# Layer 1's branch gates as 512-column products with the low blocks beside the high ones

## The reference, cut to what matters

```python
proj = h @ w_in[l]
...
def merge_branches(gate_in, y_att, y_conv, y_sc, w_o):
    g_att, g_conv, g_sc = jnp.split(jax.nn.sigmoid(gate_in), N_BRANCH, axis=-1)
    return (g_att * y_att + g_conv * y_conv + g_sc * y_sc) @ w_o
...
x = x + g1 * merge_branches(proj[..., SC_END:GATE_END], att, y_conv, y_sc, w_o[l])
```

## Time and profile before

| | us |
|---|---|
| median of three runs | 1224.73 |
| profiled execution | 1224.44 |
| its span | 1222.7 |
| TensorE busy | 1202.3 (98%) |
| VectorE busy | 864.9 (71%) |
| ScalarE busy | 530.0 (43%) |
| GpSimd busy | 190.4 (16%) |

### The profile page before, as it was taken

How to read it: one execution, slowest core, us unless ns; L and a number is a source line. 1 busy time by engine, 2 the same in 40 slices (tenths; PEclk the granted TensorE clock), 3 DMA queues, 4 the chain that set the end, 5 groups by cost and what they waited for, 6 DMA issues and landing times.

```text
span 1222.7 us, 17823 instructions
## 1 busy us (share of the span) xinstructions
PE 1202.3 (98%) x6842; PEld 1000.4 (82%) x6842; DVE 864.9 (71%) x1286; ACT 530.0 (43%) x891; POOL 190.4 (16%) x158
## 2 busy tenths in 40 slices
PE   7999999999999999999999999999999999999997
PEld 5677777788888898888888888889879998888886
DVE  4665866586877487678755665789887877766666
ACT  4342555522433352312232222465664555655554
POOL 0005994000001200000000000302980002000000
PEclk9999999999999999999999999999999999999999
DMA  9947322134464536557664665335434674676662
GB/s 297 314 142 216 84 54 69 35 87 121 120 172 124 169 92 198 159 156 215 185 201 144 211 195 161 93 98 147 124 111 115 168 209 141 195 200 189 181 198 88
DMA packets 265252, 188.88 MB, mean 154 GB/s; under 512 B 16035, under 2 KB 250833, under 8 KB 265169
## 3 DMA queue, kind: packets, MB, share of 16 engines
q1 hardware_dynamic: 264832, 187.60, 52.6%
q10 hardware_dynamic: 337, 0.15, 0.0%
HBM read 186.67 MB, written 1.05 MB: 154 GB/s over the span
## 4 chain that ended last, share of the span: by engine, by line
PE 87%; DVE 4%; ACT 3%; DMA 2%; issue 1%; DVEq 0%; ACTq 0%; SPq 0%
PE bank L2075 17%; PE bank L2077 17%; PE bank L2076 17%; PE bank L2116 5%; PE bank L2114 3%; PE scores L2563 3%; PE bank L2543 2%; PE bank L2545 2%; PE bank L2544 2%; PE probsT L2572 2%; PE attended L2586 1%; ACT Whi L401 1%; DMA Wraw<-in_w_in 1%; DVE Wlo L412 1%; PE bank L2642 1%
## 5 line engine op out<-in xcount | busy, mean ns | idle before, releaser
L412 DVE TENSOR_TENSOR Wlo<-Wraw,Whi 128x1024 fp32r<-128x1024 f32 (+3 forms) x294 | 321.7, 1103 | 105.4 <-ACT Whi L401 104.3
L401 ACT ACTIVATE Whi<-Wraw 128x1024 fp32r<-128x1024 f32 (+1 forms) x296 | 270.3, 928 | 127.0 <-PE bank L2077 71.6
L2075 PE MATMUL bank<-Hhi,Whi 128*128 128x512 f32 (+1 forms) x786 | 285.9, 364 | 0.4
L2076 PE MATMUL bank<-Hlo,Whi 128*128 128x512 f32 (+1 forms) x786 | 282.1, 359 | 0.0
L2077 PE MATMUL bank<-Hhi,Wlo 128*128 128x512 f32 (+1 forms) x786 | 282.0, 359 | 0.0
L2075 PEld LDWEIGHTS bank<-Hhi,Whi 128*128 128x128 f32 x786 | 148.6, 189 | 29.1 <-issue 6.4
L2076 PEld LDWEIGHTS bank<-Hlo,Whi 128*128 128x128 f32 x786 | 148.6, 189 | 22.3 <-issue 1.0
L2077 PEld LDWEIGHTS bank<-Hhi,Wlo 128*128 128x128 f32 x786 | 148.6, 189 | 21.9
L2075 PE MATMUL bank<-Uhi,Whi 128*128 128x512 f32 (+1 forms) x350 | 128.5, 367 | 0.2 <-issue 0.2
L2077 PE MATMUL bank<-Uhi,Wlo 128*128 128x512 f32 (+1 forms) x350 | 126.8, 362 | 0.0
L2076 PE MATMUL bank<-Ulo,Whi 128*128 128x512 f32 (+1 forms) x350 | 126.7, 362 | 0.0
(11 more groups left out here) (305 smaller groups left out, 1979.4 us busy)
## 6 DMA issues: line engine op xcount, KB each, us to landing
Wraw<-in_w_ff SPq DMA_DIRECT2D x126, 512.0 KB, 3.9
Wraw<-in_w_in SPq DMA_DIRECT2D x78, 512.0 KB, 4.0
ATT<-in_w_mod SPq DMA_DIRECT2D x58, 512.0 KB, 4.5
Wraw<-in_w_o SPq DMA_DIRECT2D x16, 512.0 KB, 4.0
ACC<-in_w_mod SPq DMA_DIRECT2D x14, 512.0 KB, 4.6
Wraw<-in_w_mla_o SPq DMA_DIRECT2D x8, 512.0 KB, 4.1
ATT<-in_w_mod SPq DMA_DIRECT2D x12, 256.0 KB, 7.6
Wraw<-in_w_kv_b SPq DMA_DIRECT2D x12, 256.0 KB, 3.7
```

The costliest lines, as they stand in the source:

```text
L401: last = act.activation(hi, raw, ACT.Copy)
L412: last = eng.tensor_tensor(lo, raw, hi.bitcast(F32), ALU.subtract)
L2075: pe.matmul(dst, sh, mh, start=j == 0, stop=False)
L2076: pe.matmul(dst, sh, ml, start=False, stop=False)
```

## The change

In layer 1 only: ScalarE copies the eight low blocks of `h` into the second half of `Hhi`, two blocks an instruction, one instruction at each of the four steps of the attention's output product. TensorE's gate tiles become `tile_beside` tiles, 8 matmuls of 512 columns and 8 of 256 in place of 24 of 256. ScalarE copies the second half of the bank to `TG`'s second half, VectorE adds the bank's first half, and ScalarE takes the tanh of that sum into `TG`'s first half. The tanh of g0 stands behind ScalarE's `look` for g1, the tanh of g1 behind the copy of g1.

```diff
@@ ScalarE
                 for m in range(4):
+                    if l:
+                        act.activation(Hhi[:, 2 * m:2 * m + 2, half[1]], Hlo[:, 2 * m:2 * m + 2, half[0]].bitcast(F32),
+                                       ACT.Copy).then_inc(beside, 1)
...
+                def gate_side(j):
+
+                    t = at.tile()
+                    act.wait_ge(tile_done, t.done)
+                    act.activation(TG[:, j, half[1]], banks[t.bank][:, half[1]], ACT.Copy).then_inc(side_done, 1)
+                    return t
+
+                def gate_tanh_out(t, j):
+
+                    act.wait_ge(drained[t.bank], t.drained)
+                    act.activation(TG[:, j, half[0]], TG[:, j, half[1]], ACT.Tanh, scale=0.5).then_inc(branch_tanh, 1)
...
-                    before = outs[-2:]
+                    before, gates = outs[-2:], []
                     for j in range(2):
                         look(next(nxt))
+                        if j and l:
+                            gate_tanh_out(gates[0], 0)
                         if before:
                             act.wait_ge(drained[before[j].bank], before[j].drained)
-                        copy_out(TG[:, j, 0:TQ], TQ, ACT.Tanh, 0.5)
+                        if l:
+                            gates.append(gate_side(j))
+                        else:
+                            copy_out(TG[:, j, 0:TQ], TQ, ACT.Tanh, 0.5)
                         if j == MEAN_AFTER[l] and mean:
                             mean()
                         if j == 0 and squares:
                             squares()
+                    if l:
+                        gate_tanh_out(gates[1], 1)
@@ VectorE
                     for j in range(2):
                         look_and_fold(next(nxt))
                         gates.append(at.tile())
+                        if l:
+                            dve.wait_ge(side_done, sides.next())
+                            dve.tensor_tensor(TG[:, j, half[1]], banks[gates[j].bank][:, half[0]], TG[:, j, half[1]],
+                                              add).then_inc(drained[gates[j].bank], 1)
...
-                        dve.wait_ge(drained[gates[j].bank], gates[j].drained)
+                        if l:
+                            dve.wait_ge(branch_tanh, tanhs.next())
+                        else:
+                            dve.wait_ge(drained[gates[j].bank], gates[j].drained)
@@ TensorE
                     for j in range(2):
-                        tile_of(P, DT, H, 0, TQ)
+                        if l:
+                            pe.wait_ge(beside, 4)
+                            tile_beside()
+                        else:
+                            tile_of(P, DT, H, 0, TQ)
```

More of the change, by code:

```diff
@@ L330, in build @@
         side_done = sem("side_done")
+        beside = sem("beside")
+        branch_tanh = sem("branch_tanh")
         value_gated = sem("value_gated")
@@ L1745, in _ @@
                 outs = []
+                sides, tanhs = Tally(), Tally()
                 looked = 0
@@ L1893, in hidden_block @@
                     low(Ulo[:, u, 0:TQ], PR[:, j, 0:TQ], Uhi[:, u, 0:TQ])
-                sides = Tally()
                 def gate_sum(j, free):
```

## The result

The changed kernel takes 1230.18 us (median of five runs, 1229.62 to 1231.65) against 1224.73 of the kernel before (1224.48 to 1225.72): 5.45 us more, ratio 1.0044 with a 95% interval of 1.0033 to 1.0055. The forecast was 1230.6, slower. The profiled execution took 1229.62 us, the shortest of the five; its span is 1227.8 us, 5.1 more than before.

What follows compares the result with a forecast made beforehand. TensorE, busy 98%, bounds the kernel; its 1.3 us saving would vanish inside waits for VectorE and ScalarE, whose shifts reach 6.2 us at the second output block. So 1224.44 + 6.2 = 1230.6 us, range 1228 to 1232.7.

Steps and rivals of the forecast that it cites:

- copies beside: Four ScalarE copies in the attention's output product, inside its waits for TensorE: cost 0; bare, 2.5 us.
- scaling of ACC: VectorE's last instruction before the mean over channels, groups 0 and 1: from 958.11 to about 959.4, shift 1.3 us.
- low weights of group 4, shift of its tile: VectorE's low weights for g0 of group 4 move from 970.86 to 973.7; TensorE's tile starts 2.8 us later.
- one loop, groups 5 to 7: VectorE and ScalarE's loop per group: 6.7 us, 0.5 more if a load is late, then 7.4 and 7.4.
- low part of the second output block: VectorE's instruction that TensorE's second output block waits for: from 1001.60 to 1007.8, total shift 6.2 us.
- term of 0.5 us for a late load: In the first of three loops of groups 5 to 7: 0.5 us more where a load lands late.
- term of 0.08 us a tile: TensorE's gate tiles fall from 2.88 to 2.80 us: 0.08 a tile, 1.3 us for the stage's 16.
- after it nothing is changed: After the branches' output product, which waits for VectorE and ScalarE in the same order, nothing changes.
- (A): Rival: TensorE keeps the bound, adds and tanhs lie in VectorE's and ScalarE's idle time; 1223.1 us, chance 0.10.
- (B): Rival: late mean, cheaper chain through g1's tanh, only VectorE's own order counts; 1226.0 to 1227.2 us, chance 0.17.
- the detour: g1's next weight copy queues behind ScalarE's tanh, which waits for VectorE's sum: 1.2 us each time.
- (C): Rival: loads come to bound, groups 4 to 7 each wait 0.5 to 1 more; 1232.6 to 1234.6 us, chance 0.13.

Runs made afterwards that it cites:

- no_low_sum: The changed kernel with ScalarE's tanh straight from the bank's first half and no VectorE sums, low operand's part left out: 1224.01 us against 1225.25 before.
- fitted_product: As fitted, but VectorE takes the convolution's product ahead of group 3's second output; operand copies stay: 1224.21 us against 1224.63 before.
- tanh_late: The changed kernel with ScalarE's tanh of g1 moved behind the next group's g1 weight copy: 1225.88 us against 1225.25 before.
- before_fitted: The kernel before with only the respread taps and split normalisation on VectorE, none of the change: 1225.62 us against 1224.97 before.
- fitted: The change with g1's tanh behind the weight copy, two taps ahead of the sum, taps respread, normalisation split: 1225.23 us against 1224.97 before.
- fitted_conv: As fitted, with VectorE's convolution product ahead of group 3's second output and ScalarE's operand copy behind group 4's weight copies: 1225.21 us against 1224.76.

## Why the prediction was right

The forecast held by its own steps, which can be read against the trace after, since the stretch starts within 0.06 us of where it did.

| step of the prediction | forecast | measured |
|---|---|---|
| gate tile | 2.80 | g0 2.81, g1 2.78 (940.40, 943.21, 945.99) |
| copies beside | in ScalarE's waits, last ends 938.9 | ends 938.71 |
| first taps | after 943.9 | 944.17 |
| scaling of ACC | 959.4 | 959.19 |
| low part of g1's weights, group 3 | 966.7 | 966.51 |
| reciprocal | 970.45 | 970.23 |
| low weights of group 4, shift of its tile | 973.7, 2.8 | 973.46, 2.65 |
| ScalarE idle ahead of g1's tanh | up to 2.7 | 2.75 |
| branch operand's tile | 981.8 | 981.55 |
| low weights of group 5, shift | 982.8, 4.4 | 982.56, 4.20 |
| low part of g1's weights, group 5 | 985.8 | 985.56 |
| one loop, groups 5 to 7 | 6.7 or 7.2, 7.4, 7.4 | 6.72, 7.38, 7.37 |
| low part of the second output block | 1007.8, shift 6.2 | 1007.03, shift 5.43 |

*The copies cost nothing.* They took 0.61 to 0.63 us each, 2.5 in all, and ScalarE's wait for TensorE in that place fell from 7.0 to 4.9 us; the last is done at 938.71, 1.7 us before the first gate tile. The first and the last of the four in ScalarE's timeline:

```profile
931.01 0.63 ACT L1036 ACTIVATE Hhi<-Hlo 128x512 fp32r<-128x512 f32 x1
...
938.10 0.61 ACT L1036 ACTIVATE Hhi<-Hlo 128x512 fp32r<-128x512 f32 x1
```

*What was mis-sized.* The term of 0.5 us for a late load in the first of the three loops didn't come: no wait of ScalarE for a load is left between 972 and 1008, where the kernel before had four from 972 to 1003; the chunks are copied later than before, and find their loads landed. The three loops took 21.47 us, not 22.0. With the 0.2 us by which each earlier step was early this makes the 0.8 of 6.2 that is missing.

*What the tiles save.* The term of 0.08 us a tile held. In TensorE's timeline the first group's two gate tiles take 5.59 us (940.40 to 945.99), where they took 5.76 (940.46 to 946.22): 0.085 a tile. First the end of before, then the changed kernel:

```profile
946.22 0.28 PE L2075 MATMUL bank<-Uhi,Whi 128*128 128x256 f32 x1
```

```profile
940.40 0.40 PE L2142 MATMUL bank<-Hhi,Whi 128*128 128x512 f32 x1
...
943.21 0.40 PE L2142 MATMUL bank<-Hhi,Whi 128*128 128x512 f32 x1
...
945.99 0.28 PE L2104 MATMUL bank<-Uhi,Whi 128*128 128x256 f32 x1
```

A whole group falls from 7.20 us to 7.01 (940.40 to 947.41), so eight groups would give 1.5 us if nothing were waited for; no_low_sum gets 1.05 of it. (*The Trainium skill (TensorE: Matmul & The Clock Gate, "Back-to-back issue gap") would give 0.02 a tile by its isolated gap, an estimate; the tile distances here give some four times as much.*) In the changed kernel all of it is lost in waits.

*What was not forecast.* Ahead of the mean, the gate row's second half waited 0.24 us for a bank that VectorE's late `G += Z` frees. The mean itself moved by 1.07 (958.78 to 959.85), not by 1.3, because the scaling of ACC that it waits for moved by 1.08 (958.11 to 959.19). And "after it nothing is changed" left out the 0.35 us that come back at a tile of the FFN.

*The rivals.* (A) would hold if TensorE kept the bound; fitted_product comes nearest to that, and gives 0.4 in the medians and 0.8 in the stage where (A) had 1.3. (B) put only VectorE's own order on the path, 1.6 to 2.8 us over the kernel before: tanh_late takes the detour out and lands at +0.63 in both counts, under that range. Counted without the form's 1.05, which is in it, VectorE's own order costs some 1.7 us there, and the detour 4.9 more. (C) is excluded by the missing load waits.

*Where luck has a part.* By the steps the forecast was too high: by 0.8 at the second output block, and by 1.0 for the profiled execution, from which it was summed (1230.6 against 1229.62). That it meets the median within 0.5 us is owed in part to the changed kernel's profiled execution being the shortest of five, 0.56 under their median.

*The waits as a sum.* Taken from the distances of matmul starts, TensorE is held 1.78, 0.92, 0.81 and 1.45 us at the last four waits, each 0.15 to 0.16 more than the idle time that the rows give: idle time counts from the modelled end of the matmul before, 0.28 after its start, where the next could have started after 0.12. That is 4.96, of which 0.27 stood before too; around the gate row and the mean 1.45 is added, which makes 6.1. Less 1.5, what the tiles save where nothing waits, 4.6 of the 5.49 are told. The rest is in tiles that start late or follow a late start. Where TensorE had waited for low weights the first gate tile takes 2.99 and 3.00 us, not 2.81 (974.78 to 977.77, 983.89 to 986.89), 0.37 in all, and smaller steps of up to 0.1 at other tiles of the stage make up the other 0.5. The rows name no wait for any of this, and its cause is not shown.

What stays open: by how much a version of fitted_product with more rounds beats the kernel before; the stage says 0.77, the medians 0.42 with an interval of some 1.1 to either side. And why the whole profiled span of before_fitted is 3.1 us longer than before's, when its stage is 1.0 longer: 2.5 of it lie ahead of the stage, which starts at 931.37 there and at 928.85 before. Its profiled execution is its longest, and its median is 0.65 above.

## What to carry to other kernels

When a result is handed from ScalarE to VectorE and back, look at what stands behind the waiting instruction on each queue before counting instructions: here 32 small instructions more cost 0.3 to 0.6 us of the stage in the better orders (77.16 against 76.88 without them, in an order of its own; 78.25 against 77.64 in the same order), and the place of one tanh ahead of a weight copy cost 4.9 us. Put the waiting instruction behind the work that others need sooner, and read the other engine's idle time in front of that work (here 1.43 us each round) as the sign. And follow the trace to the stage's end before pricing a reordering: twice here (fitted, fitted_conv) a wait that was removed came back at a later operand.

## What the runs showed of the hardware

Plain copies need no other activation table than the square root's: after the root ScalarE copies a low sum (968.96) and weights (969.24) without a load, and a load of 1.28 us comes only ahead of the next tanh, at 970.31; the tanh starts 0.01 us after its end. Two gate tiles of 8 matmuls of 512 and 8 of 256 columns take 5.59 us, two of 24 of 256 columns 5.76, so one matmul of 512 columns saves (5.76 - 5.59) / 16 = 0.011 us over two of 256. And two reorderings that each left the number of instructions as it was (fitted, fitted_conv) moved waits of 0.4 to 1.2 us from one tile to another and changed the stage by only 0.23 and 0.12.
